# Mixture-of-experts stage of a two-layer encoder: expert outputs kept in four PSUM banks, rows gathered from x itself, two more places for weights

## The reference

```python
h = modulate(rms_norm(x, norm1_g[i]), sh1, sc1)
proj = h @ w_in[i]
...                                    # Hyena branch and dilated attention, gated and merged
x = x + g1[:, None, :] * (merged @ w_out[i])

h = modulate(rms_norm(x, norm2_g[i]), sh2, sc2)
x = x + g2[:, None, :] * grouped_moe(h, router_w, router_bias, moe_w1[i], moe_w3[i], moe_w2[i])
...
def grouped_moe(...):                  # gates: the best group of four experts, the two best in it
    for e in range(N_EXPERTS):
        a = jax.nn.silu(t @ w1[e]) * (t @ w3[e])
        y = y + gates[:, e:e + 1] * (a @ w2[e])
```

## Time and profile before

| | us |
|---|---|
| median of 3 runs | 1049.43 (1048.52 to 1051.4) |
| the profiled execution's own time | 1049.43 |
| its span, first to last instruction | 1047.6 |
| TensorE busy | 997.7 (95%) |
| VectorE busy | 564.1 (54%) |
| HBM read | 329.47 MB |

### The profile page before, as it was taken

The page is one execution under the profiler, slowest core; times in us unless marked ns, Lnnn a source line. Parts: engine busy times, 40 slices in busy tenths (PEclk is TensorE's granted clock), DMA queues, the critical chain, the costliest instruction groups (busy, mean ns, idle before and its releaser), DMA issues.

```text
span 1047.6 us, 18346 instructions
## 1 busy us (share of the span) xinstructions
PE 997.7 (95%) x7709; PEld 602.5 (58%) x7709; DVE 564.1 (54%) x1192; ACT 188.5 (18%) x395; POOL 40.5 (4%) x83
## 2 busy tenths in 40 slices
PE   7999999999999999998999999999999999999794
PEld 4788567557775344443358866765878534444321
DVE  4669794868786223361235779572758622233112
ACT  4031001311233031011131110122123301110102
POOL 2100100010000000000010010001000000000000
PEclk9999999999999999999999999999999999999997
DMA  9999856297976999999999884628875599999991
GB/s 310 387 381 332 280 172 232 85 330 278 418 292 224 421 386 421 420 421 421 420 388 375 291 311 162 222 71 288 301 286 213 200 420 420 421 419 421 421 417 71
DMA packets 91883, 333.94 MB, mean 319 GB/s; under 512 B 5740, under 2 KB 6059, under 8 KB 66965
## 3 DMA queue, kind: packets, MB, share of 16 engines
q1 hardware_dynamic: 87937, 323.56, 79.3%
q0 software_dynamic: 2976, 7.19, 2.3%
q10 hardware_dynamic: 884, 1.97, 0.6%
HBM read 329.47 MB, written 1.05 MB: 316 GB/s over the span
## 4 chain that ended last, share of the span: by engine, by line
PE 78%; DVE 8%; DMA 6%; SPq 3%; issue 2%; ACT 1%; DVEq 0%; ACTq 0%
PE bank L833 76%; DMA ring<-in_moe_w_dram 4%; SPq L732 3%; DMA ring<-in_w_ada_dram 2%; PE bank L1345 1%; PE bank L1121 1%; DVE wide L2018 0%; DVE area L2014 0%; DVE wide L1807 0%; PE bank L1174 0%; DVE x L2234 0%; PE bank L895 0%; DVE area L2233 0%; DVE area L2210 0%; DVE wide L2019 0%
## 5 line engine op out<-in xcount | busy, mean ns | idle before, releaser
L833 PE MATMUL bank<-ring,hT 128*32 128x512 f32 (+3 forms) x1808 | 283.8, 555 | 9.8 <-DMA ring<-in_moe_w_dram 7.0
L833 PE MATMUL bank<-hT,ring 128*32 128x256 f32 (+1 forms) x2112 | 211.8, 380 | 0.1
L833 PEld LDWEIGHTS bank<-ring,hT 128*32 128x32 f32 (+2 forms) x1808 | 120.8, 134 | 144.8 <-issue 139.6
L833 PEld LDWEIGHTS bank<-hT,ring 128*32 128x32 f32 (+1 forms) x2112 | 157.6, 132 | 52.2 <-issue 5.5
L833 PE MATMUL bank<-ring,area 128*32 128x512 f32 (+1 forms) x744 | 117.8, 566 | 1.3 <-ACT area L1681 0.9
L833 PE MATMUL bank<-area 32*64 32x64 f32 (+5 forms) x648 | 89.1, 363 | 0.0
L1807 DVE SCALAR_TENSOR_TENSOR area<-ring,wide,area 128x512 f32<-128x512 f32 x114 | 85.3, 748 | 2.7
L2442 DVE TENSOR_TENSOR area<-bank,area 128x512 f32<-128x512 f32 x14 | 9.7, 691 | 130.4 <-PE bank L833 130.4
L833 PE MATMUL bank<-wide,hT 128*32 128x512 f32 (+1 forms) x376 | 75.1, 574 | 0.0
L833 PEld LDWEIGHTS bank<-ring,area 128*32 128x32 f32 (+1 forms) x744 | 43.6, 120 | 53.7 <-issue 48.6
L833 PEld LDWEIGHTS bank<-area 32*64 32x64 f32 (+4 forms) x648 | 37.9, 145 | 45.7 <-issue 44.4
(11 more groups left out here) (300 smaller groups left out, 1077.7 us busy)
## 6 DMA issues: line engine op xcount, KB each, us to landing
ring<-in_moe_w_dram SPq DMA_DIRECT2D x136, 1024.0 KB, 16.5
ring<-in_w_ada_dram SPq DMA_DIRECT2D x24, 2048.0 KB, 15.0
ring<-in_w_in_dram SPq DMA_DIRECT2D x24, 2048.0 KB, 12.3
wide<-in_moe_w_dram SPq DMA_DIRECT2D x32, 1024.0 KB, 12.8
cst<-in_moe_w_dram SPq DMA_DIRECT2D x13, 1024.0 KB, 14.9
area<-in_moe_w_dram SPq DMA_DIRECT2D x11, 1024.0 KB, 19.5
ring<-in_w_out_dram SPq DMA_DIRECT2D x4, 2048.0 KB, 8.5
ring<-in_w_br_h_dram SPq DMA_DIRECT2D x4, 1536.0 KB, 6.7
```

Source lines behind the costliest of these rows:

```text
L833: return pe.matmul(dst, lhsT, rhs, start=start, stop=stop, skip_group_check=True)
```

## The change

- **PSUM.** `scatter` no longer closes a sum each step: banks 2 to 5 (`out_bank`) collect all seven steps (start at step 0, stop at step 6), and VectorE adds them to x once, at the end of the stage. `accumulate` is gone. Gather, up, turn and down of a step share two banks (`step_bank`: 0 and 1 in even steps, 6 and 7 in odd ones). The taps, rates and spectra of the next layer use the pair that is free in their step, and their waits are changed to fit; the taps are spread over two spots of a step, and the second four spectra come ahead of the scatter.
- **Gather from x.** The stationary operand is now x itself, every eighth column, and `rs` goes into the entries of `sel`. The copy on ScalarE (L1659) is gone. The first `sel` is made by four operations of 128 x 64 instead of one of 128 x 256, and `sel` of a later step by two of 128 x 128 instead of one of 128 x 256.
- **Two more half places.** `XN` is the whole tile `xn`, free when the last product of `seven` is done. `PIECES` has two pieces of 512 KB, one in the second half of `hT` and one in `area` (room made by taking out `selh`, `sil` and one half of `yS`), free when the router's products are done; it is loaded by two transfers. Both join the round behind the others.
- Semaphores are merged to stay within their number, and the branch for overflowing experts, not taken here, is moved ahead of the four additions to x.

```diff
-        hg = hT[:, :, 0:P]
+        hT_flat = hT[:, :, :].rearrange("p k n -> p (k n)")
+        hg = hT_flat[:, 0:ND * P].rearrange("p (k s) -> p k s", k=ND)
...
+        halves += [(hT_flat[:, ND * P:2 * ND * P], area[:, AREA - 6 * W:AREA - 4 * W]),
+                   xn[:, :, :].rearrange("p t d -> p (t d)")]
...
                         if L + 1 == DEPTH:
                             free.insert(12, (ROWS, None))
+                        free += [(XN, None), (PIECES, None)]
...
+        def step_bank(s, n):
+            return bank[(0, 6)[s % 2] + n]
+
+        def out_bank(tt, h):
+            return bank[2 + 2 * tt + h]
...
+                    elif u == XN:
+                        sp.wait_ge(p_sev, (L * SEVEN + 6) * 7)
+                    elif u == PIECES:
+                        sp.wait_ge(p_part, (L + 1) * NT)
...
+                def gather_into(s):
+                    for k in range(ND):
+                        for tt in range(NT):
+                            last = mm(step_bank(s, k // 4)[:, (k % 4) * P:(k % 4 + 1) * P],
+                                      x[:, tt, :].rearrange("p (m k) -> p k m", k=ND)[:, k, :],
+                                      sel[:, tt, :], tt == 0, tt == NT - 1)
+                        yield k, last
+
                 def gather(s):
                     pe.wait_ge(v_sel, L * STEPS + s + 1)
-                    if s >= 2:
-                        pe.wait_ge(v_acc, (L * STEPS + s - 2) * 4 + 2)
-                    for k in range(ND):
-                        for tt in range(NT):
-                            last = mm(bank[2 + k // 4][:, (k % 4) * P:(k % 4 + 1) * P], xn[:, tt, k * P:(k + 1) * P],
-                                      sel[:, tt, :], tt == 0, tt == NT - 1)
...
                         for h in range(2):
+                            if (part, h) == (0, 1):
+                                pe.wait_ge(a_selT, n + 1)
...
-                            mm(bank[2 + 2 * tt + h][:, :], selT[:, tt * P:(tt + 1) * P],
-                               yS[:, h * W:(h + 1) * W], True, True).then_inc(p_sc, 1)
+                            mm(out_bank(tt, h)[:, :], selT[:, tt * P:(tt + 1) * P], yS[h], s == 0, s == STEPS - 1)\
+                                .then_inc(p_sc, 1)
...
                 for s in range(STEPS):
-                    if s:
-                        pe.wait_ge(a_selT, L * STEPS + s)
                     up(s, 0)
                     next_filter(s, 0)
                     if s == STEPS - 1:
                         scatter(s - 1)
                     up(s, 1)
+                    next_filter(s, 1)
                     if 0 < s < STEPS - 1:
                         scatter(s - 1)
                     turn(s)
                     if s < STEPS - 1:
                         gather(s + 1)
-                    next_filter(s, 1)
                     down(s)
...
-                for tt in range(NT):
-                    last = sc.activation(xn[:, tt, :].rearrange("p (k m) -> p k m", k=ND),
-                                         x[:, tt, :].rearrange("p (m k) -> p k m", k=ND), ACT.Copy,
-                                         scale=rs[:, tt:tt + 1])
-                last.then_inc(a_score_xn, 1)
...
-                dv.tensor_tensor(halves(sel), counted, first_two(pos_), ALU.is_equal).then_inc(v_sel, 1)
-                dv.wait_ge(v_sel, L * STEPS + 1)
-                link(dv.tensor_tensor(halves(selg[0]), halves(sel), first_two(gate_), ALU.mult))
+                def first_two(dst, scales):
+                    for tt in range(NT):
+                        for j, e in enumerate(FIRST):
+                            last = dv.tensor_scalar(dst[:, tt, j * CAP_FIRST:(j + 1) * CAP_FIRST], iota[:, 1:CAP_FIRST + 1],
+                                                    rb[pos_][:, tt, e:e + 1], scales(tt, e), ALU.is_equal, ALU.mult)
+                    return last
+
+                first_two(sel, lambda tt, e: rs[:, tt:tt + 1]).then_inc(v_sel, 1)
+                link(first_two(selg[0], lambda tt, e: rb[gate_][:, tt, e:e + 1]))
...
-                def accumulate(s):
...
-                            dv.tensor_tensor(x[:, tt, cols], x[:, tt, cols], bank[2 + 2 * tt + h][:, :], ALU.add)\
-                              .then_inc(v_acc, 1)
...
-                        dv.tensor_tensor(yS[:, cols], bank[6 + h][:, :], g2b[:, cols], ALU.mult).then_inc(v_yS, 1)
-                accumulate(STEPS - 1)
-
-                dv.wait_ge(v_acc, (L + 1) * STEPS * 4)
+                        dv.tensor_tensor(yS[h], step_bank(s, h)[:, :], g2b[:, cols], ALU.mult).then_inc(v_yS, 1)
+
                 with dv.If(over > 0):
...
+                for tt in range(NT):
+                    for h in range(2):
+                        cols = slice(h * W, (h + 1) * W)
+                        dv.wait_ge(p_sc, ((L + 1) * STEPS - 1) * 4 + 2 * tt + h + 1)
+                        dv.tensor_tensor(x[:, tt, cols], x[:, tt, cols], out_bank(tt, h)[:, :], ALU.add).then_inc(v_acc, 1)
                 dv.sem_inc(v_layer, 1)
```

More of the change, by code:

```diff
@@ L77 @@
 EXTRA = 2 * RING
-TABLE, TAIL, ROWS = EXTRA + 4, EXTRA + 5, EXTRA + 6
+TABLE, TAIL, ROWS, PIECES, XN = range(EXTRA + 4, EXTRA + 9)
 LAST = {(0, EXTRA): 3, (0, EXTRA + 1): 3, (0, EXTRA + 2): 1, (0, EXTRA + 3): 1, (1, EXTRA + 2): 3, (1, EXTRA + 3): 3}
@@ L408, in trunk_kernel @@
         mask = cst[:, C_MASK:C_MASK + NT * KEYS].rearrange("p (t n) -> p t n", t=NT)
-        slot_in = [sem(f"slot_in{u}") for u in range(ROWS + 1)]
+        slot_in = [sem(f"slot_in{u}") for u in range(XN + 1)]
         p_ada = sem("p_ada")
@@ L574, in place_blocks @@
                         u, old = free.pop(0)
+                    if u == PIECES:
+                        landings[u] += 16
                     plan[key] = halves[u], u, landings[u] + 16, [old]
@@ L598, in slot, with half_row @@
             return space, slot_in[u], value
+        def half_row(space, k, f):
+            if isinstance(space, tuple):
+                per = 2 * W // f
+                space, k = space[k // per], k % per
+            return space[:, k * f:(k + 1) * f]
         def released(L, kind, b, half):
@@ L651, in nyquist_after, with taps_in @@
             return L == 0 and c == FILTER_C + 4
-        def taps_in(L, s):
-            first = 4 * (s - TAPS_STEP)
-            return range(first, first + 4) if L + 1 < DEPTH and s in (TAPS_STEP, TAPS_STEP + 1) else ()
+        def taps_in(L, s, spot):
+            first = 4 * (s - TAPS_STEP) + 2 * spot
+            return range(first, first + 2) if L + 1 < DEPTH and s in (TAPS_STEP, TAPS_STEP + 1) else ()
         def tap(l, i):
@@ L730, in _ @@
                     name, order = ("moe_w1", "moe_w3", "moe_w2")[m], "(p k) f -> p k f"
-                    part = slice(half * (NF if m == 2 else ND) // 2, (half + 1) * (NF if m == 2 else ND) // 2)
-                    sp.dma_start(dst.rearrange("p (k f) -> p k f", f=D if m == 2 else FE),
-                                 t[name][L, experts[e], :, :].rearrange(order, p=P)[:, part, :]).then_inc(landing, 16)
+                    rows, f = ((NF if m == 2 else ND) // 2, D if m == 2 else FE)
+                    spaces = dst if isinstance(dst, tuple) else (dst,)
+                    count = rows // len(spaces)
+                    for i, space in enumerate(spaces):
+                        first = half * rows + i * count
+                        sp.dma_start(space.rearrange("p (k f) -> p k f", f=f),
+                                     t[name][L, experts[e], :, :].rearrange(order, p=P)[:, first:first + count, :])\
+                          .then_inc(landing, 16)
                 elif L == 0 and (kind == "rest" or (kind == "in" and b * 4 < AHEAD)):
@@ L917, in taps @@
                         pe.wait_ge(v_kt, i - 1)
-                    elif l and i >= 4:
-                        pe.wait_ge(v_kt, l * 12 + i - 3)
+                    elif l and i % 4 >= 2:
+                        pe.wait_ge(v_kt, l * 12 + i - 1)
                     first = (0, FOLD)[lt] if b == 0 else (1, P)[lt]
@@ L1334, in up @@
                         for j in range(4):
-                            last = mm(bank[which][32 * j:32 * j + 32, :], hg[:, k, 32 * j:32 * j + 32],
-                                      ws[TILES[s][j]][:, k % (ND // 2), :], k == 0, k == ND - 1)
+                            last = mm(step_bank(s, which)[32 * j:32 * j + 32, :], hg[:, k, 32 * j:32 * j + 32],
+                                      half_row(ws[TILES[s][j]], k % (ND // 2), FE), k == 0, k == ND - 1)
                         if k == ND // 2 - 1:
@@ L1344, in turn @@
                     for f in range(NF):
[L1345 removed]
+                        last = pe.transpose(step_bank(s, 0)[:, f * P:(f + 1) * P], act[:, f::NF], ident)
                     last.then_inc(p_actT, 1)
                     for tt in range(NT):
[L1348 removed]
+                        last = pe.transpose(step_bank(s, 1)[:, tt * P:(tt + 1) * P], selg[s % 2][:, tt, :], ident)
```

(18 more changed lines are left out.)

198 lines of the change are left out of this document (78 added, 120 removed).

## The result

The changed kernel takes 1092.56 us in the median (1090.78 to 1093.4) against 1049.43 of the kernel before: a ratio of 1.0408, 95% interval 1.0392 to 1.0423. It is 43 us slower where the forecast had 9 us faster. The profiled execution spans 1090.8 us (before 1047.6).

A forecast was written before the change was run, and what follows sets the result against it. TensorE bounds the stage at first, weights later. Each layer -5.0 + 0.4, together -9.1 from 1049.4, gives 1040.3 us; the likeliest case's own range is 1039 to 1043, the whole range 1038.5 to 1084.

The forecast's parts named there:

- The gather: Stage's gather matmuls, reading every eighth column of x: costs nothing more, judged by `turn_x` transposes (load 192 ns, spacing 110).
- `class_values`: Stepped matmul, 64 columns, 194 ns against 137 neighbouring: either each column takes twice as long, or side-by-side loads share one limit.
- Rival 1: Stepped loads cost each gather 3.33 us more: +18.7 in layer 0, +13.1 in layer 1, 1081 us; break-even spacing 145 ns; chance 0.42.
- The two places: Two added half places for expert weights: transfers of 5.0 us fall into empty queue time, gaining 5.0 us in each layer.
- The first `sel`: Start of each layer's first gather: four operations totalling 0.85 us replace one of 0.42, 0.43 us more a layer, +0.9 together.
- Accumulation in PSUM: Stage's sum over steps: takes 24 additions of 0.69 us a layer from VectorE, for which TensorE waited nowhere; worth nothing.
- The spread taps: VectorE's decayed taps between its product and next rows, covered by scatter and turn: nothing; uncovered, 1 us in each of two steps.

## Why the prediction was wrong

- *The gather* is the step that failed: "By this row the gather costs nothing more ... I take the first row, same tile, same step and same width". The row is of a transpose, and its 192 ns were compared with the 192 ns of a plain float32 matmul's load, which was chance. The trace of before allowed the right comparison, with a transpose of neighbouring columns; that of `xn` in the first part of a layer reads 128 x 128 of them:

```profile
L895 PEld LDWEIGHTS bank<-cst,xn 128*128 128x128 f32 x32 | 3.5, 144 | 1.5 <-issue 0.8 <-DVE xn L1826 0.6
```

It takes 144 ns, and `turn_x` itself took 141 once its columns stood side by side. The step thus cost that transpose 51 ns of load, hidden in its spacing, and it costs a matmul 335 - 192 = 143 ns, which shows: 238 ns a matmul instead of 112.
- *`class_values`* was the row of the right kind, and it pointed the right way. Of its two readings the first is right: with two strips side by side the loads run at twice the rate, so they share no limit.
- *Rival 1* had the mechanism, its place and its sum; its price was mis-sized, 3.33 us a gather against 4.05 measured. With 4.05 its own formulas give 7 x 4.05 - 4.6 = 23.75 in layer 0 and 7 x 4.05 - 10.2 = 18.15 in layer 1, together 41.9; with the 1.3 us of the opening that is the 43.2 measured. The spacing lies far above its break-even of 145 ns. The range's upper end rested on that price, so it ended at 1084.
- *The two places* were right in sum, 5.0 in layer 0 (4.9 measured) and 5.0 in layer 1 (4.4), as the kernel with neighbouring columns shows at 1041.3. Not seen was that layer 0 needs one place alone, and that in the changed kernel neither counts, since a slow gather had already taken the loss away.
- *The first `sel`* came as worked out: 0.43 us more a layer was forecast, about 0.45 measured. The four operations take 0.98 us, 0.13 more than the 0.85 that I had added up:

```profile
321.30 0.98 DVE L2346 TENSOR_SCALAR area<-cst,area,rs 128x64 f32<-128x64 f32 x4
```

- *Accumulation in PSUM* was put at nothing, and the kernel with it alone is at 1.0006. The spread taps, also put at nothing, cost 0.2 us in each of two steps.
- *What hides a load.* The Trainium skill, SBUF — State Buffer (section "Door 1: The DMA port swizzle"), says that SBUF has 16-byte lines, that full bandwidth needs at least two accesses to a line, and that crossing to a new one costs. For TensorE this is borne out by the steps 1 to 4 above: two columns a line (step 2) are nearly free, and beyond that a float32 matmul's operand costs 1.8 to 1.86 ns a line. The Trainium skill, TensorE: Matmul & The Clock Gate (section "LDWEIGHTS (loading the stationary operand)"), counts columns only, so a stepped load would take as long as a plain one, 192 ns here; 335 were measured. The forecast went with the second because one row agreed.

## What to carry to other kernels

Before a matmul's fixed operand is read with a step, compare the row of a stepped load with a plain load *of the same kind of instruction*, and not with another that happens to have the same number; a longer load that is hidden in one kind's spacing may be bare in the other's. If the step can't be avoided, keep it at two float32 elements, or cut the operand into two strips that load side by side; a copy on an idle engine was cheaper still here (1043.1 us against 1045.9 and 1047.6). A longer lead of transfers pays only as long as the transfers are what is late: price the change's other parts first, since 4 us more of TensorE in each step made both places worth nothing.

## What the runs showed of the hardware

- The load of a float32 matmul's fixed operand, 128 columns: 192, 196, 261, 330, 321, 318 and 335 ns at column step 1, 2, 3, 4, 5, 6 and 8; spacing 112 (115 in the first gather), 118, 173, 233, 226, 224 and 238 ns.
- The same load hardly depends on the granted clock: 338 ns at 0.50 of 2.4 GHz and 335 at full clock, in one gather at step 8.
- Strips of one operand load independently: matmuls with the operand at step 8 follow each other after 238 ns whole, 122 ns as pairs of two strips, and 109 ns as groups of four.
- Transposes with the same stepped operand load in 192 ns and neighbouring ones in 141, and both follow each other after some 110 ns. Why a float32 matmul's load takes longer than a transpose's of the same operand, no run here shows.
- With two of an expert's three matrices moved in pieces of 4 KB instead of 8 KB, the stream ran at 412 instead of 420 to 421 GB/s.
- A kernel with 1344 more TensorE instructions had a stand of 4.55 us between the layers that no other kernel has, for a gather as fast as the best.
